# A first feed-forward up product as seven block products, with its weight splits on ScalarE and VectorE

## The reference

```
m = silu(cvec) @ w_ada + b_ada                 # 9 x 1024 values, for c and for c_ctx
u = rmsnorm(h, g_pre) * (1 + scale) + shift    # 768 tokens x 1024
a, b = split(u @ w13)                          # 1024 -> 2 x 2816
h = h + 0.5 * gate * rmsnorm((silu(a) * b) @ w2, g_post)
```

## Time and profile before

| | |
|---|---|
| median of three runs | 2737.47 us |
| profiled execution, its span | 2732.5 us |
| PE busy | 2583.3 us, 95% |
| VectorE, ScalarE, GpSimd busy | 1166.0, 757.4, 1322.8 us |
| tiles 1 to 10 of the up product, with conditioning | 60.4 to 265.2 us |
| first down half | 265.2 to 359.6 us |
| tiles 11 to 21 | 359.6 to 542.7 us |
| second down half | 542.7 to 634.6 us |

### The profile page before, as it was taken

The page is one execution under the profiler, slowest core; times in us unless marked ns, Lnnn a source line. Parts: engine busy times, 40 slices in busy tenths (PEclk is TensorE's granted clock), DMA queues, the critical chain, the costliest instruction groups (busy, mean ns, idle before and its releaser), DMA issues. The chain is left out here.

```text
span 2732.5 us, 36022 instructions
## 1 busy us (share of the span) xinstructions
PE 2583.3 (95%) x14430; PEld 2204.8 (81%) x14430; DVE 1166.0 (43%) x1704; ACT 757.4 (28%) x1216; POOL 1322.8 (48%) x425
## 2 busy tenths in 40 slices
PE   7999999998999999998999998999989999969997
PEld 5888888887899788876888886878887898857775
DVE  5112101167764553026111215364435144359997
ACT  5111001135120432105100104334431012127774
POOL 1343455441563047673777775555427776610000
PEclk8999999999999999999999998999999999979999
DMA  7443121123321022232223224120012322539994
GB/s 296 185 185 144 65 77 61 62 97 118 111 77 64 1 96 77 77 142 78 92 79 113 87 84 192 64 76 1 1 63 93 124 93 93 185 130 395 374 373 172
DMA packets 52850, 334.60 MB, mean 122 GB/s; under 512 B 6660, under 2 KB 7684, under 8 KB 20016
## 3 DMA queue, kind: packets, MB, share of 16 engines
q1 hardware_dynamic: 51136, 327.02, 32.2%
q0 software_dynamic: 1584, 5.78, 0.5%
HBM read 314.41 MB, written 22.07 MB: 123 GB/s over the span
## 5 line engine op out<-in xcount | busy, mean ns | idle before, releaser
L186 POOL TENSOR_TENSOR whi<-raw,one_col 128x2048 fp32r<-128x2048 f32 (+2 forms) x155 | 515.8, 3328 | 857.9 <-PE bank L206 767.7
L189 POOL TENSOR_TENSOR wlo<-raw,whi 128x2048 fp32r<-128x2048 f32 (+2 forms) x155 | 676.7, 4366 | 12.1
L204 PE MATMUL bank<-uh_a,whi 128*128 128x512 f32 (+1 forms) x704 | 239.1, 340 | 0.0
L205 PE MATMUL bank<-ul_a,whi 128*128 128x512 f32 (+1 forms) x704 | 237.8, 338 | 0.0
L206 PE MATMUL bank<-uh_a,wlo 128*128 128x512 f32 (+1 forms) x704 | 237.5, 337 | 0.0
L3938 DVE TENSOR_TENSOR moe_wl<-moe_raw,moe_wh 128x2048 fp32r<-128x2048 f32 x84 | 189.4, 2282 | 7.2 <-DMA xs_scratch<-moe_tok,moe_dest 5.4
L3874 ACT ACTIVATE moe_wh<-moe_raw 128x2048 fp32r<-128x2048 f32 x84 | 159.8, 1912 | 25.6 <-PE bank L3849 19.7
L204 PEld LDWEIGHTS bank<-uh_a,whi 128*128 128x128 f32 x704 | 134.3, 191 | 18.3 <-issue 4.1
L204 PE MATMUL bank<-uh_b,whi 128*128 128x512 f32 x352 | 138.9, 394 | 8.1 <-DVE ul_b L1066 7.1
L206 PEld LDWEIGHTS bank<-uh_a,wlo 128*128 128x128 f32 x704 | 134.2, 191 | 14.3
L205 PEld LDWEIGHTS bank<-ul_a,whi 128*128 128x128 f32 x704 | 134.3, 191 | 14.0
(11 more groups left out here) (633 smaller groups left out, 6366.0 us busy)
## 6 DMA issues: line engine op xcount, KB each, us to landing
moe_raw<-moe_w_dram SPq DMA_DIRECT2D x84, 1024.0 KB, 7.4
cond_ring<-w_ada_dram SPq DMA_DIRECT2D x27, 1024.0 KB, 7.0
raw<-gu_a_dram SPq DMA_DIRECT2D x22, 1024.0 KB, 6.9
raw<-gu_b_dram SPq DMA_DIRECT2D x22, 1024.0 KB, 4.9
raw<-wqkv_dram SPq DMA_DIRECT2D x12, 1024.0 KB, 4.8
raw<-dn_a_dram SPq DMA_DIRECT2D x16, 704.0 KB, 4.1
raw<-dn_b_dram SPq DMA_DIRECT2D x16, 704.0 KB, 4.1
n_ada<-w_ada_dram SPq DMA_DIRECT2D x9, 1024.0 KB, 21.6
```

The lines of the kernel that those rows point to most:

```text
L186: e.nc.gpsimd.tensor_tensor(e.whi[p][:, 0:f], e.raw[p][:, 0:f], e.one_col[:, 0:1].to_broadcast([P, f]), ALU.mult).then_inc(e.w_hi, 1)
L189: e.nc.gpsimd.tensor_tensor(e.wlo[p][:, 0:f], e.raw[p][:, 0:f], e.whi[p][:, 0:f].bitcast(F32), ALU.subtract).then_inc(e.w_split, 1)
L204: e.nc.tensor.matmul(out, wh, xh, start=first, stop=False)
L205: e.nc.tensor.matmul(out, wh, xl, start=False, stop=False)
```

## The change

The hidden tiles are done in five groups of 4, 4, 4, 5 and 5 tiles, each with its down product, which adds into y from the second group on. `ffn` is no longer used for the first feed-forward; a class `SevenFeed` has the five programs.

The up product of one slot is a product of a 2 x 2 block matrix of weights (rows: a or b; columns: lower or upper four k tiles) with a 2 x 2 block matrix of inputs (upper or lower four k tiles; first or second 384 tokens). It is made as seven block products (P1 to P7) and sums of blocks, instead of eight. Each block product is a unit of 4 k tiles x 3 passes = 12 matmuls of 384 columns. Tile 0 is still made the old way (`pe_first`).

- Input sums: three sums T1 to T3 of input blocks and a fourth, from 16 subtractions of 128x384 on VectorE, each split again by ScalarE (high) and VectorE (low), once, at the start.
- Weight sums: four operations of 128x512 on VectorE for each tile (`weight_sums`), in place in the raw buffer but for one.
- Splits: the two split buffers become a ring of 8 pieces of 512 columns. ScalarE copies the high part of unit q+7 (`part_high`) and VectorE subtracts for the low part (`part_low`) while PE is at unit q. GpSimd splits no weights here, except the slot after the block, and that after the last down unit.
- Results: VectorE adds up U = s1 + P6, U7 = U + P7, U7 + P5, U7 + P4 and U + P3 from PSUM; each must be made before PE writes its bank again.
- Conditioning: 28 pieces in halves of 512 KB, loaded by GpSimd's queue; PE does a half product after unit 4s, the other after 4s+2 and the turn after 4s+3. The ninth piece of the first norm is among them, so that has eight.
- `FirstNorm` modulates x in place, without its ring of four temporaries.

```diff
-STREAM = [("gu_a0", HTILES, 16), ("dn_a0", 8, HTILES), ("gu_a1", HTILES, 16), ("dn_a1", 8, HTILES),
+GROUPS = (4, 4, 4, 5, 5)
+DOWN_TILES = {4: 4, 5: 2}
...
+S_P1, S_P6, S_P2, S_P7, S_P5, S_P4, S_P3 = range(7)
...
+    # Conditioning.pe(pe, t), called after each unit t
+        s, phase = t // self.PERIOD, t % self.PERIOD
+        if s >= self.LATE:
+            return
+        if phase in (0, 2):
+            h = phase // 2
+            pe.wait_ge(self.landed[h], 16 * s + 16)
+            if h == 0 and s >= 2:
+                pe.wait_ge(self.mixed, s - 1)
+            self.half_product(self.e.bank[6 + s % 2][:, 0:SLOT], self.ring[h], h).then_inc(self.used, 1)
+        elif phase == 3:
+            pe.wait_ge(self.parted, s + 1)
+            self.turn(self.e.bank[6 + s % 2][:, SLOT:SLOT + 4], self.part[s % 2]).then_inc(self.turned, 1)
...
+    # SevenFeed.pe, an up unit
+                if j == S_P1 and s >= 2:
+                    pe.wait_ge(*self.freed(s - 2))
+                if j == S_P2:
+                    pe.wait_ge(self.s1_ready, n)
+                if j == S_P5:
+                    pe.wait_ge(self.u_ready, n)
+                if j == S_P4:
+                    pe.wait_ge(self.u7_ready, n)
+                if j == S_P3:
+                    pe.wait_ge(self.c22_ready, n)
...
+    # a down unit
+                if k0 == 0:
+                    pe.wait_ge(*self.freed(s - 2))
+                    if i == 0:
+                        pe.wait_ge(*self.freed(s - 1))
...
+    def weight_sums(self, dve, q):
...
+        if j == S_P1:
...
+            V.tensor_tensor(self.S[:, :], a21, a22, ALU.add).then_inc(self.w_mixed, 1)
+            dve.wait_ge(self.w_mixed, before + 1)
+            V.tensor_tensor(a21, a11, a21, ALU.subtract).then_inc(self.w_mixed, 1)
+        if j == S_P6:
+            dve.wait_ge(self.w_mixed, before + 2)
+            dve.wait_ge(*self.split_of(base + S_P1))
+            V.tensor_tensor(a11, self.S[:, :], a11, ALU.subtract).then_inc(self.w_mixed, 1)
+        if j == S_P3:
+            dve.wait_ge(self.w_mixed, before + 3)
+            dve.wait_ge(*self.split_of(base + S_P2))
+            V.tensor_tensor(a12, a12, a11, ALU.subtract).then_inc(self.w_mixed, 1)
...
+    # SevenFeed.dve before its loop
+        self.weight_sums(dve, 0)
+        self.part_low(dve, 0)
+        t_sums(1, 0)
+        t_sums(3, 0)
+        t_sums(2, 1)
+        self.weight_sums(dve, 1)
+        t_low(2, 0)
+        self.part_low(dve, 1)
+        self.part_low(dve, 2)
+        t_low(3, 4)
+        self.weight_sums(dve, 6)
+        self.part_low(dve, 3)
+        t_sums(4, 9)
+        t_low(1, 8)
+        dve.wait_ge(self.sil_a, 1)
+        V.tensor_tensor(v[:, 0:T], sil[:, 0:T], e.bank[1][:, :], ALU.mult)
...
+    # SevenFeed.dve, its loop
+        for q, (kind, g, j, _, at) in enumerate(self.units):
+            if q + AHEAD < len(self.units):
+                nj = self.units[q + AHEAD][2]
+                if nj in (S_P1, S_P6):
+                    self.weight_sums(dve, q + AHEAD)
+                self.part_low(dve, q + AHEAD)
+                if nj == S_P2:
+                    self.weight_sums(dve, q + AHEAD + 4)
+            if kind == "up":
...
+                if j == S_P6:
+                    dve.wait_ge(self.s1_ready, n)
+                    dve.wait_ge(*self.done_of(q))
+                    V.tensor_tensor(self.U[:, :], self.s1[:, :], b, ALU.add).then_inc(self.u_ready, 1)
...
+                if j == S_P3:
+                    dve.wait_ge(*self.done_of(q))
+                    V.tensor_tensor(sil[:, high], self.U[:, :], b, ALU.add).then_inc(e.acc_free, 1)
+                    dve.wait_ge(self.c22_ready, n)
+                    dve.wait_ge(self.sil_b, n)
+                    V.tensor_tensor(v[:, high], v[:, high], sil[:, high], ALU.mult).then_inc(self.v_b, 1)
+                    dve.wait_ge(self.hi_b, n)
+                    V.tensor_tensor(hl[:, high], v[:, high], hh[:, high].bitcast(F32), ALU.subtract
+                                    ).then_inc(self.hid_ready, 1)
...
-        ffn(e, "fa", "gu_a", "dn_a", W, HTILES, uh, ul, y, MAIN + 73728, front=n1, late_load=(xr, dram["x"], loaded),
-            cond=e.cond, sums=sums)
+        SevenFeed(e, uh, ul, y, n1, e.cond, xr, loaded, sums).program()
```

More of the change, by code:

```diff
@@ L200, in pe_slot_begin, with three_pass @@
         pe.wait_ge(e.acc_free, g - 1)
[L203 to L206, removed]
+def three_pass(e, out, wh, wl, xh, xl, first, last, more=False):
+    e.nc.tensor.matmul(out, wh, xh, start=first, stop=False, skip_group_check=more)
+    e.nc.tensor.matmul(out, wh, xl, start=False, stop=False, skip_group_check=more)
+    return e.nc.tensor.matmul(out, wl, xh, start=False, stop=last, skip_group_check=more)
 def pe_feature_major(e, p, kt, ntile, xh, xl, ctx, between=None, ready=None, half=None, weights=None):
@@ L320, in first_gains @@
         return last
[L322 to L362, removed]
+    def half_product(self, out, w, h):
+        for k in range(KT // 2):
+            q = 32 * k
+            last = self.e.nc.tensor.matmul(out[q:q + 32, :], self.SC[:, KT // 2 * h + k, :], w[:, k * SLOT:(k + 1) * SLOT],
+                                           start=h == 0, stop=h == 1)
+        return last
@@ new lines, in act, with dve @@
+    def act(self, act, t):
+        s, phase = t // self.PERIOD, t % self.PERIOD
+        if s >= self.LATE or phase != 2:
+            return
+        act.wait_ge(self.used, 2 * s + 2)
+        if s >= 2:
+            act.wait_ge(self.turned, s - 1)
+        self.e.nc.scalar.activation(self.part[s % 2][:, :], self.e.bank[6 + s % 2][:, 0:SLOT], ACT.Copy
+                                    ).then_inc(self.parted, 1)
+    def dve(self, dve, t):
+        s, phase = t // self.PERIOD - 1, t % self.PERIOD
+        if not 0 <= s < self.LATE or phase != 0:
+            return
+        dve.wait_ge(self.turned, s + 1)
+        self.shift(EARLY + s, 1, self.e.bank[6 + s % 2][:, SLOT:SLOT + 4]).then_inc(self.mixed, 1)
+        if s == self.LATE - 1:
+            dve.wait_ge(self.mixed, self.LATE)
@@ L424, in pe @@
         pe.wait_ge(self.params_in, 48)
-        for n, r in enumerate(self.order[:-1]):
+        for n, r in enumerate(self.order):
             pe.wait_ge(self.landed[r], 16)
@@ L436, in pe @@
         turn(3)
[L438 to L446, removed]
     def act(self, act):
@@ L1169, in tile_at, with ffn @@
     return t[:, i, :] if isinstance(i, int) else t[:, ds(i, 1), :].rearrange("p a w -> p (a w)")
-def ffn(e, name, up, down, w, htiles, uh, ul, y, hid_at, front=None, late_load=None, cond=None, sums=None):
+def ffn(e, name, up, down, w, htiles, uh, ul, y, hid_at, front=None, sums=None):
     st = Stage(e, name)
@@ L1221, in _ @@
             pool.wait_ge(e.w_split, 2)
-            feed_pool(e, pool, (pool_span[0] + (front is not None and cond is None), pool_span[1]))
+            feed_pool(e, pool, (pool_span[0] + (front is not None), pool_span[1]))
         @block.tensor
@@ L1277, in silu_slot @@
                     nc.scalar.activation(tile_at(hh, i), v[p][:, :], ACT.Copy).then_inc(hi_ready, 1)
-                g0, g1 = START[f"{up}{half}"]
-                if cond is not None and half == 0:
-                    for g in range(g0, g1):
-                        slots(act, g, g + 1, silu_slot)
-                        if 1 <= g - g0 <= cond.steps + 1:
-                            cond.act(act, g - g0)
-                else:
-                    slots(act, g0, g1, silu_slot)
+                slots(act, *START[f"{up}{half}"], silu_slot)
             if sums is None:
@@ L1313, in mul_slot @@
                                             ).then_inc(lo_ready, 1)
-                g0, g1 = START[f"{up}{half}"]
-                if cond is not None and half == 0:
-                    for g in range(g0, g1):
-                        if g - g0 == 1:
-                            front.dve_late(dve)
-                        if 1 <= g - g0 <= cond.steps + 1:
-                            cond.dve(dve, g - g0)
-                        slots(dve, g, g + 1, mul_slot)
-                else:
-                    slots(dve, g0, g1, mul_slot)
+                slots(dve, *START[f"{up}{half}"], mul_slot)
                 def out_slot(nm, i, p, g, ih, gh):
```

427 lines of the change are left out of this document (366 added, 61 removed).

## The result

The changed kernel takes 2756.97 us (median of 4 runs, 2754.7 to 2759.86), the kernel before 2736.89 in runs on the same chip. The ratio is 1.0074, with a 95% interval of 1.006 to 1.0088: slower by 0.7%, clear of the noise, and by 20 us where 23 were forecast. The profiled execution took 2757.02 us and spans 2755.2; the one of before spans 2732.5.

A forecast was written before the change was run, and what follows sets the result against it. The prediction took TensorE (PE), busy 95% of the span, to bound the kernel. Its terms, -43.7 + 24.3 + 1 + 4 + 8.5 + 6.1 + 20.9 + 2 = +23.1 us, gave 2760 us, range 2733 to 2780.

The forecast's parts named there:

- The array time: Up product: 84 matmuls of 384 columns a tile, 14.57 us instead of 16.65, saving 43.7 us over 21 tiles.
- Conditioning: Up product: 28 slots split into two half products and a turn each cost 63.8 us instead of 39.5, +24.3.
- Tile 1's start: Start of the up product: PE waits for ScalarE's s1 copy and VectorE's sums, tile 1 ending near 86, +8.5 us.
- The steady chain: Up tiles without conditioning: VectorE's chain of 14.8 us against PE's 14.57, +1 us; unit boundaries +4 more.
- Rival D: VectorE paces the up product at 16.2 us a tile, giving 2774 us; chance 0.12.
- Starts of down products: First output of four down groups waits 1.5 us each for the last up product's bank, +6.1 us in all.
- The last down product: VectorE's chain of 7.9 us an output paces it instead of PE, +20.9 us; POOL's split beside it +2.
- Behind it: From the last output's add to the end of the span: time unchanged, no term.
- The median: Whole kernel: forecast span 2755.6 plus the earlier 5.0 us between median and span, giving 2760 us.
- Rival E: Conditioning halves on POOL's queue come late, each slot waiting 2.3 us, +64, giving 2824 us; chance 0.05.

The follow-up runs named there:

- e5: The changed kernel with tile 1's s1 copy and sums U and U7 put ahead of other work on their engines; 2760.73 us against 2756.97.
- e4: The changed kernel with a down product's first output no longer waiting for the bank of the last up tile; 2750.9 us against 2756.97.
- e2: The changed kernel with VectorE adding an output's running sums one output later in the last down product; 2751.03 us against 2756.97.
- e3: The changed kernel with running sums of outputs 2 to 6 in the last down product over 8 of 768 columns; 2740.34 us against 2756.97.
- e6: The changed kernel with the last down product's third weight slot loaded before x instead of behind it; 2750.21 us against 2756.97.
- e7: The changed kernel with one conditioning insertion per slot, later sums, no last-up-bank wait, one more load before x, earlier tile 1 start; 2729.52 us against 2756.97.

## Why the prediction was right, step by step

**The array time** is right. TensorE's timeline in the changed kernel, with one half product, and then one turn, in the stream:

```profile
...
61.95 0.33 PE L208 MATMUL bank<-ul_a,seven_rh 128*128 128x384 f32 x1
62.13 0.34 PE L209 MATMUL bank<-uh_a,seven_rl 128*128 128x384 f32 x1
62.40 0.64 PE L329 MATMUL bank<-cond_ring,cond_sc 128*32 128x256 f32 x8
62.96 0.45 PE L207 MATMUL bank<-seven_th,seven_rh 128*128 128x384 f32 x1
63.25 0.34 PE L208 MATMUL bank<-seven_tl,seven_rh 128*128 128x384 f32 x1
...
100.02 0.34 PE L209 MATMUL bank<-seven_th,seven_rl 128*128 128x384 f32 x1
100.19 0.50 PE L291 MATMUL bank<-cond_ps,cond_part 128*128 128x2 f32 x4
100.55 0.42 PE L207 MATMUL bank<-uh_a,seven_rh 128*128 128x384 f32 x1
100.81 0.34 PE L208 MATMUL bank<-ul_a,seven_rh 128*128 128x384 f32 x1
...
```

61.95 to 62.13, and so on over a unit, is 0.173, where 0.1735 came from the line through two widths of the earlier trace rows. That part of the change does what it says and brings 43.7 us.

**Conditioning** is right in its mechanism and 4 us too high. From 62.13 to 63.25 are 1.12, two pitches are 0.35, so a half product costs 0.77 there and another 0.03 in the matmuls behind it, 0.80 in all; forecast 0.78. A turn that waits for nothing costs 0.45 (100.02 to 100.81, less two pitches), not 0.61: that is the number that was mis-sized. 56 half products, 28 turns and what three turns lose by finding ScalarE late (0.9 each) come to 60 us; forecast 63.8, before 39.5. 20 in place of 24.3.

**Tile 1's start** is right. TensorE and ScalarE:

```profile
...
71.06 0.66 PE L207 MATMUL bank<-uh_a,seven_rh 128*128 128x384 f32 x1 [5.71 <-ACT seven_s L1587]
...
```

```profile
...
69.18 0.84 ACT L1576 ACTIVATE seven_hh<-seven_v 128x768 fp32r<-128x768 f32 x1 [0.54 <-DVEq L1651]
69.92 0.61 ACT L1516 ACTIVATE seven_rh<-raw 128x512 fp32r<-128x512 f32 x1
70.44 0.47 ACT L1587 ACTIVATE seven_s<-bank 128x384 f32<-128x384 f32 x1
...
```

The three ScalarE operations are those of the forecast, in its order, and P2 starts at 71.06 where 70.8 was worked out. The 3 us gap that was forecast before P5 isn't there: P2 and the half product behind it ran at half clock, 5.1 us long instead of 2.75 (as from 60.21 to 62.96), and P7 then ended at 78.4, as the turn's copy on ScalarE did. Tile 1 ends at 86.1 (forecast: near 86). From its start at 60.21 that is 25.9; less its own 14.57, three half products and a turn, the start costs 8.4 (8.5 forecast): 5.9 the wait, 2.4 the half clock, 0.2 the turn. e5 shows what the forecast did not say: P2's wait covers the turn's, and both end in VectorE's list.

**The steady chain**: direction and number of tiles right, length short. VectorE, the add of P4 in two tiles without conditioning, and the windows view of the stretch between:

```profile
...
418.20 0.55 DVE L1683 TENSOR_TENSOR seven_v<-seven_s,bank 128x384 f32<-128x384 f32 x1
...
433.53 0.56 DVE L1683 TENSOR_TENSOR seven_v<-seven_s,bank 128x384 f32<-128x384 f32 x1 [0.83 <-PE bank L209]
...
```

```profile
...
418.20:433.53 15.33, 15.16 (x86) 14.44 (x85) 11.68 (x21) 6.31 (x12) 0.00 (x0) 1.00 0.20 69
...
```

The loop is 15.33 us, not 14.8. Eight tiles stand behind the last slot of conditioning, as forecast (its last turn is at 413.2). Five of them take 15.3 to 15.4; the first of the last group and the last of each group take 14.6 to 14.8. The eight, from 420.1 to 465.5 and from 509.1 to 584.5, take 4.2 us more than 8 x 14.57, the boundaries of their units included; forecast 5 for chain and boundaries. My sign for it, VectorE above 90% busy, was wrong: it is busy 11.68 of 15.33, 76%. The rest are handoffs to ScalarE (0.59, 0.66, 0.59, 0.70) and 0.83 for PE. A chain can set the pace while the engine that does most of it is idle a quarter of the time. Rival D, 16.2 a tile, falls.

**Starts of down products**: cause right, size too high. In three of four only 0.7 is lost beyond the insertion of conditioning that stands there, for PE does that while the bank comes free; in the fourth, behind the last slots, it is 1.6. Together 3.7, and e4 gives 3.5 to 4.0; 6.1 forecast. The terms for conditioning, chain and down starts were thus 4, 0.8 and 2.4 too high, 0.6 more than the stretch's 6.6; the 0.6 is spread over it in pieces whose cause stays open.

**The last down product** is the forecast's largest term and right in its mechanism: VectorE's chain paces it (e2, e3), PE waits for banks. It took 69.8 where 64.6 + 2 were forecast. One steady output, and then the one beside POOL:

```profile
...
636.76 0.68 DVE L1706 TENSOR_TENSOR y_a<-y_a,bank 128x512 f32<-128x512 f32 x1
639.94 0.96 DVE L805 TENSOR_TENSOR s_tmp_xz<-y_a,xr 128x768 f32<-128x768 f32 x1 [2.16 <-ACT y_a L788]
641.10 0.96 DVE L816 TENSOR_TENSOR s_acc_yy<-s_acc_yy,s_tmp_yy 128x768 f32<-128x768 f32 x1 [0.20 <-DVE s_tmp_xz L805]
...
643.71 0.95 DVE L816 TENSOR_TENSOR s_acc_xx<-s_acc_xx,s_tmp_xx 128x768 f32<-128x768 f32 x1
644.58 0.68 DVE L1706 TENSOR_TENSOR y_a<-y_a,bank 128x512 f32<-128x512 f32 x1
...
647.75 2.83 DVE L805 TENSOR_TENSOR s_tmp_xz<-y_a,xr 128x768 f32<-128x768 f32 x1 [2.16 <-ACT y_a L788]
...
```

```profile
...
647.41 2.35 POOL L192 TENSOR_TENSOR wlo<-raw,whi 128x1024 fp32r<-128x1024 f32 x1
...
```

636.76 to 644.58 is 7.82 (7.9 forecast), and the product beside POOL's subtraction takes 2.83 in place of 0.96, 1.9 us, once (2 forecast). The same was to be read from the earlier trace rows.
The Trainium skill (SBUF — State Buffer, section "SBUF: two separate sides") calls the shared port an exclusive lock that the other waits for through the whole instruction. By that rule the product would wait from 647.75 to POOL's end at 649.76 and end 0.96 later, at 650.72; it ended at 650.58, so the trace agrees to 0.14.
The prediction left open whether POOL's copy stops VectorE too. Here no product or sum met it (645.45 to 647.34); in e2 one did and took 2.65 us, to 0.8 after the copy's end. Meeting both instructions cost 3.8, near the term's upper bound of 4.

What failed in this term is its start. ScalarE and SyncE after the last up product:

```profile
...
584.72 0.33 SPq L1425 DMA_DIRECT2D xr<-x_dram  x1
...
585.57 3.36 SPq L172 DMA_DIRECT2D raw<-dn_a_dram  x2
```

```profile
...
597.44 0.52 ACT L1516 ACTIVATE seven_rh<-raw 128x384 fp32r<-128x384 f32 x1 [9.48 <-DMA raw<-dn_a_dram]
597.87 0.83 ACT L769 ACTIVATE s_tmp_xx<-xr 128x768 f32<-128x768 f32 x1
...
```

The forecast let x land 10.1 after the last up product, as in the earlier trace rows, and the first square follow. But the change also issues one load fewer before x: the third weight slot comes behind x, lands at 597.4, and its high part stands on ScalarE in front of the square of x, though x is there at 595.2. The round starts at 12.9, not at 10.1, and output 1's add comes at 19.1, not at 15.1; from there to the last add are 50.6 us where 51.4 were forecast. In e6, which turns those two loads round, ScalarE has the high part done and waits for x alone:

```profile
...
589.63 0.52 ACT L1516 ACTIVATE seven_rh<-raw 128x384 fp32r<-128x384 f32 x1 [1.64 <-PE bank L209]
595.04 0.85 ACT L769 ACTIVATE s_tmp_xx<-xr 128x768 f32<-128x768 f32 x1 [4.88 <-DMA xr<-x_dram]
...
```

Output 1's add is then 15.1 behind the issue of x and the last one 64.9, 4.7 less than in the changed kernel. This order of loads is a part of the change for which the forecast has no term.

**Behind it**, costed at nothing too, 3.2 us went. 1.5 are from the last add to the next block's first matmul: the granted clock is 0.5 from 649.7 to 659.9 (before it was so from 647.4 to 657.6), so that the eight mean products behind the last sums run at half clock, 0.64 us apart where they were 0.33 apart, and from the first of them to the next matmul are 6.09 in place of 4.85. The other 1.7 are in the last 2082 us, a part that takes 2080 to 2086 in the ten traces, whatever the edit: scatter.

**The median**: 2760 was forecast, 3 more than measured, though the span was met. The forecast added the 5.0 by which the median before lay above its profiled span; here it is 1.8. In the runs on record the time lies 1.8 to 1.9 above the span of the same execution. By that the profiled execution of before took 2734.3, and the other 3.2 were chance (beside e7 the kernel before took 2729.07 to 2743.19).

**Rival E**, conditioning halves late: they land in 3.9 us and PE has not one wait for them. The array's stream never stood for a transfer in the up product.
The Trainium skill (SBUF — State Buffer, the trap "DVE blocks DMA") names a VectorE operation in 2-port perf mode as what starves such transfers. While they ran, VectorE did 355 operations with two inputs and 16 copies out of PSUM, busy 204 of 351 us, and no transfer took over 6.1, so the trace agrees.

## What to carry to other kernels

Price a product that saves array time by what it makes of the stream: a product put between two matmuls of it cost its own time and 0.35 us more here, and a small turn 0.1 more, so put such things in one place. When a stage that hid a chain gets shorter, time the chain by itself: its waits on the other engine (2.17 us an output) matter more than either engine's busy share, and they are filled by moving work of the output before into them. And the order of loads is a part of the change: what is loaded behind the one transfer that a chain waits for should not be needed, on the same engine, ahead of the chain.

## What was not expected of the hardware

In the changed kernel PE stood from 65.4 to 71.1; the granted clock fell to half (1.2 GHz) at 69.4, within that gap, and rose at 76.2, so that 5 us of it lay over work. In e5 PE stood from 70.1 to 78.4; the clock was half from 75.1 to 85.3, and 7 us of it lay over work. A gap that is 2.6 us longer cost 3 us of stream, though P2 had begun 6.2 earlier. The last down product of the changed kernel, with PE idle 1.1 to 3.2 us before five of its outputs, has two more stretches at half clock, 622.4 to 625.8 and 639.4 to 642.8. They cost nothing there: PE still waits for VectorE behind each (1.1 and 9.4 us).
